# Query rotation placed a step later, key sums split by token tile, a split first output step and early first scores in a two-block transformer kernel

## The chip, the cores and the metric

The program runs on one core of a Trainium2 chip. The metric is the device time of one execution in microseconds (us); lower is better. All times below are of that core.

## What is computed

Two transformer blocks over 512 tokens of width 1024, in float32. The first has differential attention, a convolution branch and 16 experts of which each chooses its tokens. The second has an mLSTM layer, and then the layer that matters here: keys and values from a small latent vector (MLA), read by 8 heads in chunks, and a memory attention of 4 heads over 256 memory rows. The parts of the reference that the change touches:

```python
def shared_kv(x, positions, kv_norm, w_kv_a, kv_lat_norm, w_kv_b, k_gain):
    h = rmsnorm(x, kv_norm)
    c_kv, k_pe = split_cols(h @ w_kv_a, [KV_LORA, QK_ROPE])
    kv = (rmsnorm(c_kv, kv_lat_norm) @ w_kv_b).reshape(bsz, s, B_HEADS, QK_NOPE + V_HEAD)
    k_nope, v = kv[..., :QK_NOPE], kv[..., QK_NOPE:]
    k = jnp.concatenate([k_nope, jnp.broadcast_to(k_pe[:, :, None, :], ...)], axis=-1)
    k = rmsnorm(k, k_gain)
    k = jnp.concatenate([k[..., :QK_NOPE], rope(k[..., QK_NOPE:], positions)], axis=-1)
    return k, v

def mla_layer(x, positions, k_sh, v_sh, ...):
    q_lat, z, mq, mz = split_cols(h @ w_in, [Q_LORA, B_WIDTH, MEM_WIDTH, MEM_WIDTH])
    q = (rmsnorm(q_lat, q_lat_g) @ w_q_up).reshape(bsz, s, B_HEADS, QK_HEAD)
    q = rmsnorm(q, q_gain)                      # then rope on its last 64 columns
    attn = chunk_causal_attention(q, k_sh, v_sh)
    y_b = attn * jax.nn.silu(z)
    y_mem = memory_attention(mq, mz, mk, mv, mq_gain)
    return x + jnp.concatenate([y_b, y_mem], axis=-1) @ w_out
```

## The kernel before

The kernel is a sequence of stages, each a block of five instruction streams written out by hand (TensorE, VectorE, ScalarE, GpSimd, and SyncE for loads). Engines meet through semaphores inside a stage and at a barrier of all engines at its end. The last two stages matter.

**The products.** `SplitGemm` computes products in float32 quality with three faster ones: ScalarE writes the rounded operand (`highs`, L482), VectorE the rest (`lows`, L491 and L495), and TensorE multiplies high by high, high by low and low by high (`multiply`, L429). A job is one product against one block of weights; it has `k_tiles` steps of 128 rows, and units of 128 tokens or features, each with a PSUM bank. Steps of all jobs are numbered through. ScalarE and VectorE go through the same numbers (`split`), one to three steps ahead of TensorE: at each number they split the operands, then take finished units out of PSUM, then do the other work that was added for that number (`add(work, number, function)`). TensorE waits per step for the low parts (`wait_low`), and at a job's first step per unit for the bank (`wait_bank`). So the place in these lists sets the order on every engine.

**The latent stage** (`latent_stage`, barrier at L3369). Its jobs in order: the latent of keys and values (KVA, steps 0 to 7), the latent of queries (QLA, 8 to 15), four pairs of heads of keys and values (KVB + c, two steps each, 16 to 23), four pairs of heads of queries (QUP + c, three steps each, 24 to 35), the memory queries (MQ, 36 to 43), and the gates (44 to 67). Five banks, 0 to 4, go round among the units; banks 5 to 7 are for transposes. For each pair c of key heads:
- ScalarE squares the keys (L3517); VectorE sums them to 8 columns `ks[:, 0]`, 4 token tiles by 2 heads (L3675), and adds the sum of the shared rotary part `pes`, 4 columns, each for both heads (`sums_k`, L3676).
- ScalarE takes the root (L3521), VectorE inverts it (L3682, `finish_k`) and scales the rotary part (L3686); GpSimd scales the keys `kn` by it (L3747), and behind that scales up to three tiles of `xt` (L3756), the operand of the MQ job.
- TensorE transposes them (`turn_k`, L3418 and L3420) once ScalarE has taken the previous pair out (`take_k`, L3526 and L3527).

The last pair of key and value heads, KVB + 3, is taken by VectorE (L3306), with two copies per unit. For the queries, `rotate_q(c)` (four VectorE operations, L3707 to L3710) stands at the number where the job is taken, plus 1 (plus 2 for c = 0): 30, 32, 35 and 38. `sums_q(c)` (L3691) stands at plus 2, `finish_q(c)` at plus 4; TensorE turns them (`turn_q`) at plus 3.

**The attention stage** (`attention_stage`, name `ba`). It has `nu` = 48 units: 16 of memory attention, 32 of chunked attention. TensorE's loop over u issues scores of unit u (L2436), transposes of the probabilities of unit u - 4 (L2450), from u = 48 on a step of the output product, and the values product of unit u - 5 (L2460). VectorE takes the maximum (L2491), normalises (L2498) and takes the result (L2503); ScalarE does the exponential (L2550) and copies the transposed probabilities (L2535). Scores lie in banks 0, 1, 2, 7 in turn. The four first units of the output product take over these banks, so that each waits in turn for one of the last four exponentials (`bank_waits`). In the loop before:

```python
                if 4 <= u < nu + 4:
                    turn(u - 4)
                if nu <= u < nu + 4:
                    out.products(pe, start=u - nu, stop=u - nu + 1)
                if u >= 5:
                    values(u - 5)
```

Of the kernel before, what the change touches and what calls it, by code (L numbers as in the profile page):

```python
# [19 lines left out]
ALU = mybir.AluOpType  # L20
# [277 lines left out]
class SplitGemm:  # L298
# [133 lines left out]
    def products(self, pe, after=None, start=0, stop=None):  # L432

        for s in range(start, len(self.steps) if stop is None else stop):
            j, k = self.steps[s][0], self.place[s]
            job, n_units, k_tiles = self.jobs[j], self.main_units(j), self.block(j)[1]
            if k == 0 and "split_ready" in job:
                pe.wait_ge(*job["split_ready"])
            w, a = self.w_split[s % self.ns], self.split_of(s)
            self.wait_low(pe, s)  # L440
            for u in range(n_units):
                unit = self.units[self.first_unit[j] + u]
                if k == 0:
                    self.wait_bank(pe, unit)
                ins = self.multiply(pe, unit, w, a, k == 0, k == k_tiles - 1)
                if k == k_tiles - 1 and u < n_units - 1:
                    ins.then_inc(self.ready, 1)
            ins.then_inc(self.used, 1)
            for work in (after or {}).get(s, []):
                work()  # L450

    def operands(self, s):
# [1932 lines left out]


def attention_stage(m, name, units, at, st_at, y, x, out_slots, store):

# [19 lines left out]

    score_banks = (0, 1, 2, 7)
    bank_of = lambda u: score_banks[u % 4]  # L2410
# [11 lines left out]
    with nc.Block() as block:  # L2422
# [6 lines left out]
        def _(pe):  # L2429
            def scores(u):  # L2430

                if u >= 4:
                    pe.wait_ge(exped, u - 3)
                lhs, rhs = units[u]["scores"]
                alone = "turned" not in units[u]
                ins = pe.matmul(ps[:, bank_of(u), 0:units[u]["width"]], lhs, rhs, start=True, stop=alone)  # L2436
                if alone:
                    ins.then_inc(scored, 1)
# [25 lines left out]
            for u in range(nu + 5):  # L2464
# [8 lines left out]
                if 4 <= u < nu + 4:  # L2473
                    turn(u - 4)
                if nu <= u < nu + 4:
                    out.products(pe, start=u - nu, stop=u - nu + 1)
                if u >= 5:
# [4 lines left out]
        def _(dve):  # L2482
            step = m.dve_steps.on(dve)

            def head(u):
                w = units[u]["width"]
                dve.wait_ge(scored, u + 1)
                s = ps[:, bank_of(u), 0:w]
# [739 lines left out]

def latent_stage(m, x, xt, kt, kpt, qt, qpt, v, y, mqt, q_scale, slots):

# [138 lines left out]
    with nc.Block() as block:  # L3369
# [9 lines left out]
        def _(pe_):  # L3379
# [75 lines left out]
            for h in range(3):  # L3455
                add(work, taken_at(MQ) + 6, lambda h=h: turn_mq(h))
            add(work, taken_at(MQ) + 9, lambda: turn_mq(3))
            g.products(pe_, work)

# [128 lines left out]
        def _(dve):  # L3588
# [84 lines left out]
            def sums_k(c):  # L3673
                dve.wait_ge(k_squared, c + 1)
                step(nc.vector.tensor_reduce(ks[:, 0], k_junk[:], AX.X, ALU.add))  # L3675
                tt(ks[:, 0], ks[:, 0], spread(pes[:], 2), ALU.add).then_inc(k_summed, 1)  # L3676

# [54 lines left out]
            for c in range(NB):  # L3732
                add(work, taken_at(QUP + c) + (1 if c else 2), lambda c=c: rotate_q(c))
                add(work, taken_at(QUP + c) + 2, lambda c=c: sums_q(c))
# [26 lines left out]
def two_blocks(nc, dram):  # L3761
    with ExitStack() as ctx:
        ctx.enter_context(nc.allow_non_contiguous_dma("short rows of gains and gate weights"))
        m = Machine(nc, ctx, dram)
        m.gates = m.keep("gates", [CAP, NE])
        m.rows = m.keep("rows", [CAP, NE + 1], U32)
# [142 lines left out]
        q_scale = m.area("q_scale", [P, BH // 2, 4, 2], 108608)  # L3909
        latent_stage(m, x, xt, kt, kpt, qt, qpt, v, y, mqt, q_scale, m.gaps + [m.arena + 98304])  # L3910
        m.close()
# [53 lines left out]
```

## Time and profile before

| | us |
|---|---|
| median of 3 runs | 2184.02 |
| lowest and highest run | 2183.22, 2184.87 |
| the profiled execution, its own time | 2185.32 |
| its span, first to last instruction | 2183.2 |
| TensorE busy | 2157.2 |
| VectorE busy | 1653.6 |
| ScalarE busy | 1392.3 |
| GpSimd busy | 340.0 |
| TensorE clock granted (mean) | 0.999 |

PE is TensorE's multiplications, PEld its weight loads, DVE VectorE, ACT ScalarE, POOL GpSimd; a q behind a name is the engine's sequencer. L495 is line 495 of the kernel. A row of a timeline gives start, length, engine, line, operation, what it writes and reads, the shape, and how many such instructions in a row it stands for; in square brackets, where there was one, the idle time of the engine before it and who ended it. The latent stage runs from 1840 to 2033.7 in the span, the attention stage from there to the end.

### The profile page before, as it was taken

The numbers are of one execution on the slowest core, as the hardware profiler recorded it, in microseconds if no ns is written. First come the engines' busy times: TensorE is split into PE (matmuls) and PEld (weight loads), VectorE is DVE, ScalarE is ACT, GpSimd is POOL, SyncE is SP. The second block draws the span as 40 slices with busy tenths as digits, with TensorE's granted clock in tenths as the row PEclk, the third lists the DMA queues.
The fourth block names the chain that finished last, engine by engine and source line by source line (L and its number), as shares of the span: only waits on it lengthen the run. The fifth ranks groups of instructions, "written<-read, shape, count | busy, mean of one in ns | idle before, by whom it ended". The sixth has DMA issues, their size and how long they took to land. (4 is left out here: it accounts for less than half of the span.)

```text
span 2183.2 us, 31916 instructions
## 1 busy us (share of the span) xinstructions
PE 2157.2 (99%) x11509; PEld 1557.7 (71%) x11509; DVE 1653.6 (76%) x2155; ACT 1392.3 (64%) x1796; POOL 340.0 (16%) x209
## 2 busy tenths in 40 slices
PE   9999999999999999999999999999999999999999
PEld 9988765565565555655556555687897788888777
DVE  6456678998989989899898998756755556875664
ACT  5345577777777777767777777755555555676653
POOL 3032041211122111121111200330000000211000
PEclk9999999999999999999999999999999999999999
DMA  6213479999999999999999999522321131241301
GB/s 188 83 57 117 168 272 370 377 382 371 384 383 372 382 370 382 385 376 380 371 383 383 374 381 368 217 86 88 90 66 59 59 118 51 61 138 39 116 1 39
DMA packets 179672, 506.88 MB, mean 232 GB/s; under 512 B 12557, under 2 KB 57389, under 8 KB 179581
## 3 DMA queue, kind: packets, MB, share of 16 engines
q1 hardware_dynamic: 174829, 494.92, 60.8%
q0 software_dynamic: 4752, 10.75, 2.2%
q8 instruction: 57, 0.93, 0.2%
q14 instruction: 34, 0.28, 0.0%
HBM read 492.99 MB, written 10.48 MB: 231 GB/s over the span
## 5 line engine op out<-in xcount | busy, mean ns | idle before, releaser
L2252 DVE TENSOR_TENSOR pieces_low<-pieces,pieces_high 128x2048 fp32r<-128x2048 f32 x383 | 873.3, 2290 | 109.2 <-ACT pieces_high L2197 105.1
L2197 ACT ACTIVATE pieces_high<-pieces 128x2048 fp32r<-128x2048 f32 x382 | 729.1, 1917 | 237.8 <-PE ps L2121 231.2
L2121 PE MATMUL ps<-pieces_high,ex_x 128*66 128x512 f32 x2080 | 574.9, 393 | 1.1 <-PEq L1593 0.5
L2121 PEld LDWEIGHTS ps<-pieces_high,ex_x 128*66 128x66 f32 x2080 | 279.4, 136 | 195.6 <-issue 7.2
L2121 PE MATMUL ps<-pieces_low,ex_x 128*66 128x512 f32 x1040 | 323.6, 392 | 0.0
L2121 PE MATMUL ps<-pieces_high,ex_h 128*66 128x512 f32 x992 | 277.0, 393 | 0.0
L495 DVE TENSOR_TENSOR in_w<-ring,in_w 128x256 fp32r<-128x256 f32 (+2 forms) x276 | 125.1, 460 | 155.0 <-ACT in_w L482 153.1
L2593 PE MATMUL ps<-hn_split,in_w 128*128 128x512 f32 x864 | 221.3, 406 | 2.7 <-DVE in_w L495 1.6
L2121 PEld LDWEIGHTS ps<-pieces_low,ex_x 128*66 128x66 f32 x1040 | 141.6, 136 | 97.4
L482 ACT ACTIVATE in_w<-ring 128x256 fp32r<-128x256 f32 (+2 forms) x276 | 117.0, 426 | 127.2 <-PE ps L2593 57.2
L2121 PEld LDWEIGHTS ps<-pieces_high,ex_h 128*66 128x66 f32 x992 | 133.6, 136 | 90.4 <-DVE pieces_low L2252 3.2
L2593 PEld LDWEIGHTS ps<-hn_split,in_w 128*128 128x128 f32 x864 | 159.5, 188 | 44.3 <-DVE in_w L495 5.1
L429 PE MATMUL ps<-out_w,out_a 128*128 128x512 f32 x768 | 180.5, 393 | 2.2 <-DVE out_a L495 1.5
L429 PEld LDWEIGHTS ps<-out_w,out_a 128*128 128x128 f32 x768 | 142.6, 188 | 34.6 <-DVE out_a L495 3.4
L2355 POOL DMA_INDIRECT ex_rows<-xhat_scratch,ex_rows_in x15 | 110.6, 7374 | 320.3 <-DVE ex_rows_in L2258 312.8
L2361 POOL DMA_INDIRECT resid_scratch<-ex_y,ex_rows_out x15 | 73.1, 4872 | 551.3 <-DVE ex_y L2307 551.3
L2121 PE MATMUL ps<-pieces_low,ex_h 128*66 128x512 f32 x496 | 154.3, 392 | 0.0
L2121 PEld LDWEIGHTS ps<-pieces_low,ex_h 128*66 128x66 f32 x496 | 67.6, 136 | 46.8
L495 DVE TENSOR_TENSOR out_w<-ring,out_w 128x512 fp32r<-128x512 f32 x64 | 44.2, 690 | 68.9 <-ACT out_w L482 68.6
L482 ACT ACTIVATE out_w<-ring 128x512 fp32r<-128x512 f32 x64 | 40.2, 628 | 75.2 <-PE ps L429 61.3
L2601 PE MATMUL ps<-in_w,hn_split 128*128 128x256 f32 x576 | 80.4, 293 | 0.7 <-ACT mq L2665 0.7
L3747 POOL TENSOR_TENSOR kn<-kn,k_ss 128x512 f32<-128x512 f32 x8 | 11.1, 1408 | 432.2 <-DVE k_ss L3682 432.2
(510 smaller groups left out, 2777.7 us busy)
## 6 DMA issues: line engine op xcount, KB each, us to landing
pieces<-in_w_gate SPq DMA_DIRECT2D x128, 1024.0 KB, 7.3
pieces<-in_w_up SPq DMA_DIRECT2D x128, 1024.0 KB, 7.7
pieces<-in_w_down SPq DMA_DIRECT2D x128, 1024.0 KB, 8.6
ring<-in_a_w_in SPq DMA_DIRECT2D x24, 1024.0 KB, 5.2
ring<-in_b_w_in SPq DMA_DIRECT2D x4, 2048.0 KB, 7.8
ring<-in_w_in SPq DMA_DIRECT2D x7, 1024.0 KB, 4.9
ring<-in_b_w_out SPq DMA_DIRECT2D x2, 3072.0 KB, 14.3
ring<-in_w_in SPq DMA_DIRECT2D x8, 512.0 KB, 3.6
```

The lines of the kernel that those rows point to most:

```text
L429: ins = pe.matmul(self.psum(unit), lhs, rhs, start=(first and i == 0), stop=(last and i == 2))
L482: self.m.nc.scalar.activation(parts[:, 0, :], x, ACT.Copy, scale=scale).then_inc(self.high, 1)
L495: ins = self.m.nc.vector.tensor_tensor(parts[:, 1, :], x, parts[:, 0, :].bitcast(F32), ALU.subtract)
L2121: ins = pe.matmul(ps[0:CAP, banks + c, :], parts[a][:, k0 + k, :], w[b][:, k, c * 512:(c + 1) * 512], start=start and k == 0 and a == b == ...
L2197: nc.scalar.activation(m.high[:, n % NSPLIT, :], m.pieces[:, n % NPIECE, :], ACT.Copy).then_inc(high_done, 1)
L2252: nc.vector.tensor_tensor(m.low_part[:, n % NSPLIT, :], m.pieces[:, n % NPIECE, :], m.high[:, n % NSPLIT, :].bitcast(F32), ALU.subtract).t ...
L2355: nc.gpsimd.indirect_dma_start(out=xg[:], out_offset=None, in_=m.xhat[:], in_offset=bass.IndirectOffsetOnAxis(ap=rows_in[:, 0:1], axis=0)) ...
L2361: nc.gpsimd.indirect_dma_start(out=m.resid[:], out_offset=bass.IndirectOffsetOnAxis(ap=rows_out[:, 0:1], axis=0), in_=y[:], in_offset=None ...
L2593: ins = pe.matmul(psum, w[:, x, u * P:u * P + psum.shape[0]], a[:, y, :], start=(first and i == 0), stop=(last and i == 2))
L2601: ins = pe.matmul(psum[:, b, :], a[:, x, t0:t0 + P], w[:, y, 0:cols], start=(first and i == 0 and b == 0), stop=(last and i == 2 and b == ...
L3747: tt(part, part, spread(r[:, :, h], x.shape[3]), ALU.mult).then_inc(scaled, 1)
```

## The change

Four edits:
- `rotate_q(3)` stands at number 39 instead of 38, behind the splits of step 39 and ahead of `sums_q(3)`.
- `sums_k` adds the rotary sum with four tensor_scalar operations, one for each token tile, each on 2 columns with a column of `pes` as the scalar, instead of one tensor_tensor on 8 columns.
- The output product's step 0 is issued in two parts: units 0 to 2 at u = 48, unit 3 at u = 49 ahead of step 1. `products` is cut into `product(pe, s, first, stop)` for this.
- The scores of unit 0 are issued in the latent stage, behind its last product, into bank 7; the banks of the scores become 7, 0, 1, 2. A new semaphore `m.first_scored` tells VectorE of them, and `scored` counts from unit 1 on.

```diff
+    def product(self, pe, s, first=0, stop=None):
+
+        j, k = self.steps[s][0], self.place[s]
+        job, n_units, k_tiles = self.jobs[j], self.main_units(j), self.block(j)[1]
+        if k == 0 and "split_ready" in job:
+            pe.wait_ge(*job["split_ready"])
+        w, a = self.w_split[s % self.ns], self.split_of(s)
+        self.wait_low(pe, s)
+        for u in range(first, n_units if stop is None else stop):
+            unit = self.units[self.first_unit[j] + u]
+            if k == 0:
+                self.wait_bank(pe, unit)
+            ins = self.multiply(pe, unit, w, a, k == 0, k == k_tiles - 1)
+            if k == k_tiles - 1 and u < n_units - 1:
+                ins.then_inc(self.ready, 1)
+        if u == n_units - 1:
+            ins.then_inc(self.used, 1)
...
+FIRST_SCORES = 7
...
-    score_banks = (0, 1, 2, 7)
+    score_banks = (FIRST_SCORES, 0, 1, 2)
...
             def scores(u):
 
+                if u == 0:
+                    return
...
-                if nu <= u < nu + 4:
-                    out.products(pe, start=u - nu, stop=u - nu + 1)
+                if u == nu:
+                    out.product(pe, 0, stop=3)
+                elif u == nu + 1:
+                    out.product(pe, 0, first=3)
+                if nu < u < nu + 4:
+                    out.product(pe, u - nu)
...
-                dve.wait_ge(scored, u + 1)
+                dve.wait_ge(*((scored, u) if u else (m.first_scored, 1)))
...
+            def first_scores():
+                pe_.wait_ge(mq_taken, MEMH)
+                pe_.matmul(ps[:, FIRST_SCORES, 0:MEM], mqt[:, 0, 0:P], mk[:, 0, :], start=True,
+                           stop=True).then_inc(m.first_scored, 1)
+
+            add(work, len(g.steps) - 1, first_scores)
...
-                tt(ks[:, 0], ks[:, 0], spread(pes[:], 2), ALU.add).then_inc(k_summed, 1)
+                for t in range(4):
+                    ins = ts(ks[:, 0, t, :], ks[:, 0, t, :], pes[:, t:t + 1], None, ALU.add)
+                ins.then_inc(k_summed, 1)
...
-                add(work, taken_at(QUP + c) + (1 if c else 2), lambda c=c: rotate_q(c))
+                add(work, taken_at(QUP + c) + (1 if c in (1, 2) else 2), lambda c=c: rotate_q(c))
...
+        m.first_scored = m.lasting("first_scored")
```

## Rows read from the trace of the kernel before

**Rows 1.** The page's line of engines: busy us (share of the span) and number of instructions.
```profile
PE 2157.2 (99%) x11509; PEld 1557.7 (71%) x11509; DVE 1653.6 (76%) x2155; ACT 1392.3 (64%) x1796; POOL 340.0 (16%) x209
```
**Rows 2.** The timeline of TensorE in the latent stage; columns as told above.
```profile
1907.90 4.21 PE L429 MATMUL ps<-in_w,qlt 128*128 128x384 f32 x21 [0.43 <-DVE v L3306]
...
1913.93 4.47 PE L429 MATMUL ps<-in_w,qlt 128*128 128x384 f32 x24
1918.56 1.06 PE L3418 MATMUL ps<-masks,kn 128*128 128x128 f32 x8 [0.16 <-issue]
...
1940.40 5.95 PE L429 MATMUL ps<-in_w,in_a 128*128 128x512 f32 x24 [0.86 <-DVE in_a L495]
```
**Rows 3.** The timeline of all engines around the boundary of the two stages.
```profile
2030.89 2.64 ACT L3337 ACTIVATE y<-ps 128x512 f32<-128x512 f32 x4 [4.89 <-PE ps L429]
...
2033.80 1.28 ACT L2550 ACT_TABLE_LOAD   x1 [0.27 <-PEq L3369]
...
2033.83 2.58 PE L2436 MATMUL ps<-mk,mqt 128*128 128x256 f32 x10 [0.94 <-PEq L3369]
2034.54 0.86 DVE L2491 TENSOR_REDUCE ba_st<-ps 128x1 f32<-128x256 f32 x2 [7.67 <-PE ps L2436]
2035.09 0.47 ACT L2550 ACTIVATE ba_probs<-ps,ba_st 128x256 f32<-128x256 f32 x1
```
**Rows 4.** The timeline of all engines around the output product's first step.
```profile
2107.34 2.46 PE L429 MATMUL ps<-out_w,out_a 128*128 128x512 f32 x9
...
2108.68 0.48 ACT L2535 ACTIVATE ba_pt<-ps 128x384 f32<-128x384 f32 x1
...
2110.49 0.96 PE L429 MATMUL ps<-out_w,out_a 128*128 128x512 f32 x3 [0.69 <-ACT ba_probs L2550]
...
2111.29 0.60 PE L2460 MATMUL ps<-ba_pt,v 128*128 128x128 f32 x4
...
2111.97 3.02 PE L429 MATMUL ps<-out_w,out_a 128*128 128x512 f32 x12
```
**Rows 5.** VectorE at the key sums: line L3676, timeline, and one wait (total, times, longest).
```profile
L3676 DVE TENSOR_TENSOR k_ss<-k_ss,k_pe_ss x4: 169/990/1245, 1889.3 to 1913.2; 128x8 f32<-128x8 f32 x4
...
1905.72 0.99 DVE L3676 TENSOR_TENSOR k_ss<-k_ss,k_pe_ss 128x8 f32<-128x8 f32 x1
1906.64 0.55 DVE L495 TENSOR_TENSOR in_w<-ring,in_w 128x384 fp32r<-128x384 f32 x1
...
DVE k_ss L3682 <- ACT k_ss L3521: 2.5, 1, 2.5
```
**Rows 6.** The timeline of GpSimd beside the key sums of c = 2 and 3.
```profile
1905.42 1.27 POOL L3756 TENSOR_TENSOR xt<-xt,row_scales 128x512 f32<-128x512 f32 x1
1906.65 1.66 POOL L3756 TENSOR_TENSOR xt<-xt,row_scales 128x512 f32<-128x512 f32 x1
...
1914.08 1.69 POOL L3756 TENSOR_TENSOR xt<-xt,row_scales 128x512 f32<-128x512 f32 x1
```
**Rows 7.** Timelines of VectorE and GpSimd elsewhere, where both work.
```profile
1437.44 0.81 DVE L3031 TENSOR_SCALAR xl_tmp<-xl_tmp 128x16 f32<-128x16 f32 x1
...
1435.37 2.85 POOL L3221 TENSOR_SCALAR x<-fin_gained,fin_roots 128x1024 f32<-128x1024 f32 x1
...
1974.33 1.54 DVE L495 TENSOR_TENSOR in_a<-xt,in_a 128x512 fp32r<-128x512 f32 x1
1975.79 1.53 DVE L491 SCALAR_TENSOR_TENSOR in_w<-ring,cols,in_w 128x512 fp32r<-128x512 f32 x1
```
**Rows 8.** Timelines of TensorE and VectorE around the last query rotation.
```profile
1947.41 8.43 PE L429 MATMUL ps<-in_w,in_a 128*128 128x512 f32 x36
...
1948.74 0.69 DVE L495 TENSOR_TENSOR in_a<-xt,in_a 128x512 fp32r<-128x512 f32 x1
```
**Rows 9.** The timeline of ScalarE behind the key sums and copies.
```profile
1909.87 1.06 ACT L3517 ACTIVATE k_junk<-kn 128x1024 f32<-128x1024 f32 x1 [2.40 <-DVE v L3306]
...
1914.18 0.30 ACT L3521 ACTIVATE k_ss<-k_ss,eps 128x8 f32<-128x8 f32 x1 [1.19 <-DVE k_ss L3676]
```

More of the change, by code:

```diff
@@ L434, in products @@
         for s in range(start, len(self.steps) if stop is None else stop):
[L435 to L448, printed above, removed]
+            self.product(pe, s)
             for work in (after or {}).get(s, []):
                 work()
+    def product(self, pe, s, first=0, stop=None):
[14 more added lines that the diff above has]
+            ins.then_inc(self.used, 1)
     def operands(self, s):
@@ L3226, in _, with latent_stage @@
                                     ALU.mult).then_inc(s["mq_scaled"], 1)
-def latent_stage(m, x, xt, kt, kpt, qt, qpt, v, y, mqt, q_scale, slots):
+def latent_stage(m, x, xt, kt, kpt, qt, qpt, v, y, mk, mqt, q_scale, slots):
     nc, ps = m.nc, m.ps
@@ L3909, in two_blocks @@
         q_scale = m.area("q_scale", [P, BH // 2, 4, 2], 108608)
-        latent_stage(m, x, xt, kt, kpt, qt, qpt, v, y, mqt, q_scale, m.gaps + [m.arena + 98304])
+        latent_stage(m, x, xt, kt, kpt, qt, qpt, v, y, mk[1], mqt, q_scale, m.gaps + [m.arena + 98304])
         m.close()
```

## The prediction, made before the changed kernel had run

> **What bounds the kernel now.** I read the page's engine line first: TensorE is busy for 2157.2 us, so at most 26 us of this program are idle time of TensorE, and an edit can pay only where it takes a piece of these away [rows 1]. Next I read TensorE's order of time in the two stages that the diff touches, for its own waits. In the latent stage three matter: 0.43 us at 1907.90, 0.16 at 1918.56 and 0.86 at 1940.40 [rows 2]. At the boundary of the stages there is one of 0.94, and one of 0.69 in the first step of the output product [rows 3, 4]. Then I read what VectorE, GpSimd and ScalarE do ahead of each. All the rest is TensorE passing from one multiplication to the next. The profiled execution took 2185.32 us with a span of 2183.2; the median of the runs is 2184.02, 1.3 below it. The sum below is a difference within the profiled span, and I lay it on the median.
>
> **Key sums.** `sums_k(c)` ends in one addition of 8 columns. It takes 0.169 us where nothing hinders it, and 0.99 us or more in the last three of its four turns [rows 5]. The reason stands beside it: GpSimd is scaling `xt`, in instructions of 1.27 us. The addition that starts at 1905.72 ends at 1906.71, just behind GpSimd's instruction, which ends at 1905.42 + 1.27 = 1906.69 [rows 5, 6]. So the two engines share something that one of them holds for a whole instruction. The diff replaces the addition by four tensor_scalar of 2 columns each, back to back (nothing shows their spacing; at the 0.17 of the free addition, which moves as little, four take between 0.2 and 0.7, and I take 0.4).
>
> What matters is whether a tensor_scalar waits for GpSimd too. The row nearest to it says yes: 16 columns at 1437.44 take 0.81 us, where 8 columns take 0.17 when free, and end at 1438.25, where GpSimd's instruction ends at 1435.37 + 2.85 = 1438.22 [rows 7]. That row has an immediate as its scalar and another instruction on GpSimd, so it isn't proof. The Trainium skill, page Vector Engine (DVE) Microarchitecture Reference, section 5.1 Performance modes, says that a one-source operation with two fp32 elements in SBUF runs in the mode that uses both read ports, and SBUF — State Buffer, section SBUF: two separate sides, that such an operation and a GpSimd instruction lock each other out for a whole instruction. The 0.81 us agrees; no row here has 2 columns. By that rule four small instructions meet the lock four times where one addition met it once. By it the sum is the forecast's +3.1, by its opposite rival A's -0.8.
>
> How many of GpSimd's instructions do they wait for? Two rows of VectorE in a row, at 1974.33 and 1975.79, last 1.54 and 1.53 us each, where the first kind takes 0.69 when alone [rows 7, 8]: when GpSimd has its next instruction ready, it gets in between two of VectorE. Yet the L495 behind the addition starts at 1906.64, just ahead of GpSimd's next at 1906.65, and isn't held up (0.55) [rows 5, 6]. So about two short VectorE instructions pass at each change. Four tensor_scalar and the L495 behind them then pass as 2, 2, 1, over three of GpSimd's instructions instead of one.
> - c = 0: no GpSimd work runs; VectorE is 0.2 us later. TensorE has no wait nearby: nothing.
> - c = 1: the addition stands beside the second of three GpSimd instructions; one is left, 1.3 us. VectorE idles for 2.5 us before the reciprocal that follows, waiting for ScalarE [rows 5]: it covers this. Nothing.
> - c = 2: L495 starts two instructions later, 2 x 1.27 = 2.5 us. Behind it stand the eight copies that free the banks of the last key and value product. TensorE waits for them at 1907.90 already [rows 2], and ScalarE's next square has waited 2.40 us for them [rows 9]. All of the 2.5 us arrives at TensorE.
> - c = 3: two GpSimd instructions are there. The sum is ready one later, 1.27 us. ScalarE has waited 1.19 us for it at 1914.18, in front of the takes and of the turned keys for which TensorE waits at 1918.56 [rows 2, 9]. There is no slack, so 1.3 us arrive.
> Together +3.8 us.
>
> If instead the tensor_scalar doesn't wait, the gain is small: the L495 behind it has two SBUF inputs and waits for the same end, 1906.69, which is 0.05 us from where it starts now [rows 5, 6]. ScalarE gets its sum 0.6 us sooner at c = 3, but then copies four units that TensorE finishes one by one in its stretch from 1913.93, the last near 1916.2 [rows 2]. I take 0.1 us. So this edit lies between -0.1 and +3.8.
>
> **Rotation.** `rotate_q(3)` moves behind the splits of step 39. Before, these splits end at 1949.43; TensorE needs them after the first of the three steps in its 8.43 us stretch from 1947.41, at 1950.2 [rows 8]. They now end some 2 us earlier, where 0.8 of slack stood. `sums_q(3)` comes behind both, and keeps its place. The rotation ends 1.3 us later, at about 1949.4, and its reader on TensorE stands behind step 40, at 1955.7. Nothing, and the wait of 0.86 at 1940.40 belongs to `rotate_q(2)`, which isn't moved [rows 2].
>
> **First scores.** They go into the latent block. TensorE's last product there ends near 2033.83 - 0.94 = 2032.9; two short multiplications more end near 2033.4, while ScalarE's last copy ends at 2030.89 + 2.64 = 2033.53 [rows 3]. The boundary still waits for ScalarE. VectorE's first maximum can start some 0.6 us before 2034.54. But the exponential it feeds waits for the table load, 2033.80 + 1.28 = 2035.08, and starts at 2035.09 [rows 3]. VectorE's third maximum stands behind the first normalisation in the code, so nothing moves. The change of banks is a renaming. Worth 0; with bounds of -0.2 (a maximum less in the ramp) and +0.3 (TensorE late at the boundary). No DMA is moved, and the queue of the loads issues as before.
>
> **First output step in two parts.** Its fourth unit waits for the last exponential: 0.69 us idle at 2110.49; behind it come the values product of unit 43 (2111.29) and the transposes of unit 45, up to 2111.97. What they read is ready: ScalarE's copy behind the one for unit 43 already ends at 2108.68 + 0.48 = 2109.16 [rows 4]. In the change these two fill the hole. TensorE is free at 2107.34 + 2.46 = 2109.80, they take 2111.97 - 2111.29 = 0.7 us, and the fourth unit still starts at 2110.49. Step 1 starts at 2111.29 instead of 2111.97. What comes later keeps its distances and has no wait, as TensorE runs on to the end. -0.7, between 0 and -0.8.
>
> **Sum.** +3.8 + 0 + 0 - 0.7 = +3.1 us: 2184.02 + 3.1 = 2187.1.
>
> **The rivals.**
> A. The 2-column tensor_scalar doesn't wait for GpSimd. For it: it has one tensor as input, and instructions with two are what the trace mostly shows waiting. Against it: the row at 1437.44 [rows 7]. -0.1 - 0.7 = -0.8: 2183.2.
> B. They wait, but all four pass at one change. Then only L495 loses its place to one GpSimd instruction: +1.3 at c = 2, +0.2 at c = 3, -0.7: +0.8, 2184.8. For it: L495 passes right behind the addition now. Against it: the pair at 1974.33.
> C. Slower than a measurement can miss: GpSimd's instructions last 1.66 to 1.69 us, and not 1.27, wherever a VectorE instruction stands between them [rows 6]. If each change costs that, c = 2 costs 3.3 and c = 3 1.7; with 0.3 at the boundary and 0.7 back this is +4.6, 2188.6. It decides once TensorE's waits at 1907.90 and 1918.56 grow by more than 5.1 us together. Against it: the 0.4 us more are the time of the VectorE instruction itself there, and a 2-column instruction is shorter.
> D. The output step doesn't gain, as the values product waits for a VectorE row that isn't ready; +3.8, 2187.8. Speaks against it: the copy at 2108.68 ends 0.6 us before TensorE is free [rows 4].
>
> **How the numbers follow.** Forecast 0.45; A 0.27; B 0.15; C 0.07; D 0.04; 0.02 for something in the order of the program that no row shows and that gains much. The range goes from A with 0.8 us for the scatter of the runs (they span 1.65) to just short of C: 2182.4 to 2188.4. It leaves out C, the 0.02, and the tails of A and the forecast, some 0.17. 0.2% is 4.4 us, about what a measurement of this kernel can tell from no change: faster is below 2179.7, slower above 2188.4. Slower: C and a small tail of the forecast, 0.09. Faster: 0.02. Same: 0.89.
>
> **What would show each step.** Key sums: four rows in place of the addition; in the forecast the first and the third last about a microsecond each at c = 2, the L495 behind them starts near 1909.2 relative to the other rows (1906.6 in rival A), and TensorE's wait before the second unit of the first query product grows from 0.43 to about 2.9; its wait before the last turned keys grows from 0.16 to about 1.4. In rival A all four last 0.17 and the L495 takes the wait over. Output step: the 0.69 is gone and values and transposes stand between units three and four. First scores: a first maximum right behind the boundary, and an exponential that still starts with the table load's end. Rotation: no row of TensorE changes. The prediction is wrong if the sums stay short, or if TensorE's waits in the latent stage change anywhere else.

## The result, and the profile after

The changed kernel takes 2187.07 us (median of 22 runs, 2186.48 to 2189.13), the kernel before, in the same number of runs beside it, 2184.62 (2183.22 to 2186.31). The ratio is 1.0014 with an interval of 1.0008 to 1.0019: slower by 1.7 to 4.2 us, which is less than the 0.2% that the prediction took as its bound of "same". The forecast was 2187.1. Its profiled execution took 2187.21 us with a span of 2185.0; that of the kernel before took 2185.32 with 2183.2.

The page's engine line of the changed kernel stands against [rows 1]. VectorE has the twelve instructions more (2167 against 2155), and 5.2 us more of busy time, which is waiting inside the short instructions: their rows add up to 9.45 us against 3.40:

```profile
PE 2158.4 (99%) x11509; PEld 1560.2 (71%) x11509; DVE 1658.8 (76%) x2167; ACT 1393.4 (64%) x1796; POOL 338.9 (16%) x209
```

**TensorE in the latent stage** (timeline of the changed kernel), against [rows 2]:

```profile
1905.03 0.78 PE L429 MATMUL ps<-in_w,qlt 128*128 128x384 f32 x3
1908.82 6.62 PE L429 MATMUL ps<-in_w,qlt 128*128 128x384 f32 x21 [3.02 <-DVE v L3320]
1915.28 1.03 PE L3432 MATMUL ps<-masks,kn 128*128 128x128 f32 x8
...
1921.13 1.06 PE L3432 MATMUL ps<-masks,kn 128*128 128x128 f32 x8 [0.15 <-issue]
...
1942.97 5.95 PE L429 MATMUL ps<-in_w,in_a 128*128 128x512 f32 x24 [0.86 <-DVE in_a L500]
```

The wait in front of the second unit of the first query product has gone from 0.43 to 3.02 us, as forecast. But the 21 multiplications behind it now take 6.62 us where they took 4.21, and the wait before the last turned keys has not grown at all. Another wait is gone, that of 0.55 before the turned keys behind the 21 multiplications, which neither [rows 2] nor the prediction has (kernel before):

```profile
1912.67 1.06 PE L3418 MATMUL ps<-masks,kn 128*128 128x128 f32 x8 [0.55 <-issue]
```

So of the 2.41 us that the 21 multiplications lose, 1.69 reach the turned keys (distances of 6.46 and 4.77 us from the second unit). The rotation's neighbour, 0.86, is as it was.

**The key sums** on VectorE, with GpSimd and ScalarE beside them (timelines of the changed kernel), against [rows 5, 6, 9]:

```profile
1887.66 0.62 DVE L3698 TENSOR_SCALAR k_ss<-k_ss,k_pe_ss 128x2 f32<-128x2 f32 x4
...
1904.06 3.58 DVE L3698 TENSOR_SCALAR k_ss<-k_ss,k_pe_ss 128x2 f32<-128x2 f32 x4
1907.56 0.55 DVE L500 TENSOR_TENSOR in_w<-ring,in_w 128x384 fp32r<-128x384 f32 x1
1908.03 0.41 DVE L3320 COPY kn<-ps 128x256 f32<-128x256 f32 x1
...
1914.07 2.50 DVE L3698 TENSOR_SCALAR k_ss<-k_ss,k_pe_ss 128x2 f32<-128x2 f32 x4
...
1903.76 3.73 POOL L3779 TENSOR_TENSOR xt<-xt,row_scales 128x512 f32<-128x512 f32 x3
...
1913.77 2.51 POOL L3779 TENSOR_TENSOR xt<-xt,row_scales 128x512 f32<-128x512 f32 x2
...
1916.60 0.30 ACT L3542 ACTIVATE k_ss<-k_ss,eps 128x8 f32<-128x8 f32 x1 [2.70 <-DVE k_ss L3698]
```

Alone (c = 0, the first row) four additions take 0.62 us. At c = 2 they take 3.58, until GpSimd has done all of its three instructions (1903.76 + 3.73 = 1907.49), and L500 and the copies stand behind them. At c = 3 they take 2.50 us, beside two instructions of GpSimd. Taken one by one, the four of c = 2 last 0.99, 1.33, 1.31 and 0.22 us, those of c = 3 1.00, 1.32, 0.22 and 0.22: each waits for an instruction of its own as long as GpSimd has one. At c = 1, also beside GpSimd, the four take 2.75 us where the addition took 1.25; VectorE's wait for ScalarE behind them shrinks from 2.52 to 1.03 and covers that.

**The clock.** The windows of the same stretch (length, busy time of PE, PEld, DVE, ACT and POOL with counts, granted clock, share of DMA, GB/s):

```profile
1905.00:1909.00 4.00, 0.98 (x7) 0.66 (x6) 4.00 (x8) 0.71 (x2) 2.49 (x3) 0.86 0.00 0
1909.00:1914.40 5.40, 5.40 (x17) 5.40 (x18) 5.33 (x11) 3.11 (x5) 3.46 (x3) 0.50 0.10 10
1914.40:1920.00 5.60, 5.60 (x37) 5.56 (x37) 4.75 (x8) 3.31 (x8) 4.66 (x4) 0.97 0.30 99
```

In the middle window the granted clock is 0.50, the lower of the two levels (1.2 GHz in place of 2.4). The 0.86 and 0.97 beside it put the low stretch at 1907.9 to 1914.7: it began while TensorE stood in its 3.02 us wait, and lasted some 6.8 us. That is where the 21 multiplications lose their time, and no step of the prediction has it.

**The output step and the boundary** (timelines of the changed kernel), against [rows 4] and [rows 3]:

```profile
2109.95 2.45 PE L429 MATMUL ps<-out_w,out_a 128*128 128x512 f32 x9
2112.24 0.61 PE L2470 MATMUL ps<-ba_pt,v 128*128 128x128 f32 x4
2112.68 0.49 PE L2460 MATMUL ps<-masks,ba_probs 128*128 128x128 f32 x3
2113.18 3.67 PE L429 MATMUL ps<-out_w,out_a 128*128 128x512 f32 x15
2116.69 0.83 PE L2470 MATMUL ps<-ba_pt,v 128*128 128x128 f32 x6
...
2033.47 2.64 ACT L3351 ACTIVATE y<-ps 128x512 f32<-128x512 f32 x4 [4.88 <-PE ps L429]
2036.38 1.28 ACT L2564 ACT_TABLE_LOAD   x1 [0.27 <-PEq L3383]
2036.42 0.42 DVE L2505 TENSOR_REDUCE ba_st<-ps 128x1 f32<-128x256 f32 x1 [6.97 <-PEq L3383]
2037.68 0.47 ACT L2564 ACTIVATE ba_probs<-ps,ba_st 128x256 f32<-128x256 f32 x1
```

The values product and the transposes fill the hole of 0.69 us: from the first of the nine multiplications to the values product of six (2116.69 - 2109.95) it is 6.74 us. In the kernel before, the same distance is 2114.83 - 2107.34 = 7.49. At the boundary, VectorE's first maximum comes right behind the barrier, and the exponential still starts with the end of the table load, 2036.38 + 1.28.

**The sum of it.** I matched TensorE's multiplications of the two traces one by one, and read where their distance changes: +4.2 us between 1905 and 1921, -0.75 in the output step, nothing at the rotation, nothing at the boundary. That is +3.5, and yet the spans differ by 1.9. The rest, -1.7, arises about 460 us ahead of any line of the change, as the kernel before ran at half clock for a while there:

```profile
1448.00:1452.00 4.00, 4.00 (x23) 4.00 (x23) 1.11 (x6) 1.01 (x2) 0.00 (x0) 0.58 0.12 41
```

This is the kernel before; in that window the changed kernel has

```profile
1448.00:1452.00 4.00, 4.00 (x30) 3.74 (x29) 1.32 (x5) 2.29 (x5) 0.00 (x0) 1.00 0.06 21
```

The instructions are the same there, and of the thirteen kernels profiled in this study four have the lower clock in it (before, and the experiments sums_c2, sums_c3 and sums_early), nine don't, and no edit goes with it. So it differs between executions and is no part of the change, and the spans can't be compared as a whole. Below I compare stretches.

### The profile page after: what moved, and what is told of

It is laid out like the page before. It is cut to its first block and busy times, and to the rows that moved or that the text cites. A ratio compares the mean times of both kernels' runs of the same rounds, so it can differ in the third digit from the quotient of the medians.

```text
span 2185.0 us, 31930 instructions
## 1 busy us (share of the span) xinstructions
PE 2158.4 (99%) x11509; PEld 1560.2 (71%) x11509; DVE 1658.8 (76%) x2167; ACT 1393.4 (64%) x1796; POOL 338.9 (16%) x209
## 5 line engine op out<-in xcount | busy, mean ns | idle before, releaser
L500 DVE TENSOR_TENSOR in_w<-ring,in_w 128x256 fp32r<-128x256 f32 (+2 forms) x276 | 125.1, 460 | 154.2 <-ACT in_w L487 152.4
L500 DVE TENSOR_TENSOR out_w<-ring,out_w 128x512 fp32r<-128x512 f32 x64 | 44.2, 690 | 69.0 <-ACT out_w L487 68.7
```

The source lines that it names most:

```text
L500: ins = self.m.nc.vector.tensor_tensor(parts[:, 1, :], x, parts[:, 0, :].bitcast(F32), ALU.subtract)
```

## The experiments

My theory after this: (1) the key sums cost all of the loss, by the number of short instructions that meet GpSimd; (2) c = 2 costs 2.6 us through the wait, and the wait costs more through the clock; (3) the output step gives back 0.75; (4) rotation and first scores do nothing. Rivals: the sort of instruction costs, not the number; c = 3 costs as forecast and is only misplaced; the low clock is chance or comes with something other than the wait; the output step's gain needs the other edits.

The table has TensorE's time, from its timelines, between the same four points of every kernel: the start of the first unit of the first query product (1906.69 in the kernel before), its second unit (1907.90), the turned keys behind it (1912.67), and the turned keys of c = 3 (1918.56). The last columns are the medians of this kernel and of the kernel before beside it.

| kernel | to second unit | to turned keys | to those of c = 3 | sum against before | median | before |
|---|---|---|---|---|---|---|
| before | 1.21 | 4.77 | 5.89 | | | |
| after | 3.79 | 6.46 | 5.85 | +4.23 | 2187.07 | 2184.62 |
| sums_only | 3.78 | 5.62 | 6.15 | +3.68 | 2187.52 | 2184.22 |
| no_sums | 1.21 | 4.76 | 5.89 | -0.01 | 2183.52 | 2184.22 |
| sums_c2 | 3.78 | 6.47 | 5.83 | +4.21 | 2187.26 | 2184.22 |
| sums_c3 | 1.20 | 4.77 | 6.99 | +1.09 | 2185.05 | 2184.22 |
| add4 | 3.60 | 6.53 | 5.85 | +4.11 | 2187.06 | 2184.02 |
| add2 | 2.35 | 4.77 | 5.87 | +1.12 | 2185.24 | 2184.02 |
| early_scale | 1.16 | 4.77 | 5.86 | -0.08 | 2190.98 | 2184.02 |
| sums_early | 1.17 | 4.76 | 5.88 | -0.06 | 2190.18 | 2184.02 |
| fill | 3.84 | 4.77 | 7.00 | +3.74 | 2186.95 | 2184.58 |
| out_only | 1.20 | 4.77 | 5.86 | -0.04 | 2182.81 | 2184.58 |
| junk_out | 1.16 | 4.77 | 5.86 | -0.08 | 2183.45 | 2184.58 |

### The key sums alone, and all but them

sums_only is the kernel before with this edit alone:

```diff
-                tt(ks[:, 0], ks[:, 0], spread(pes[:], 2), ALU.add).then_inc(k_summed, 1)
+                for t in range(4):
+                    ins = ts(ks[:, 0, t, :], ks[:, 0, t, :], pes[:, t:t + 1], None, ALU.add)
+                ins.then_inc(k_summed, 1)
```

> The kernel before with the key sums' edit alone (four tensor_scalar). If that edit is the cause: +3.8 us by the forecast's sum (2.5 at c = 2, 1.3 at c = 3), +4.3 by the reading of the trace after (2.6 of waiting at c = 2, 1.7 because TensorE then runs at half its clock for 6.8 us, nothing more at c = 3, whose delay lies beside that). If the 2.5 us of the whole change come from another edit or from where the code lies: within 0.5 us of before.

no_sums is the changed kernel with the reverse of it, so that the three other edits stand alone.

> The changed kernel with the one addition of 8 columns put back, so with the other three edits alone. If the key sums are the whole loss: -0.7 to -0.8 us against the kernel before, all of it at the output product's first step. If the first scores or the rotation cost anything: above -0.5.

Measured: sums_only 1.0016 [1.0007, 1.0025], +3.3 us at the median; no_sums 0.9996 [0.9987, 1.0005], -0.7. In the trace of no_sums the stretch is that of the kernel before to 0.01 us, and from there to the end TensorE's distance to the kernel before changes in the output step only, by 0.73. So the sums are the whole loss, and the other three together are the output step's gain. (Further up, the low clock at 1448 that the kernel before had and no_sums had not makes 1.5 us between these two profiled executions.) sums_only shows one thing more: its low clock lasted 3.4 us and not 6.8, and began only 1.6 us behind the same wait of 3.0 (which ended at 1909.49):

```profile
1905.00:1909.00 4.00, 1.49 (x12) 1.16 (x10) 4.00 (x6) 0.65 (x2) 3.16 (x3) 1.00 0.00 0
1909.00:1914.40 5.40, 4.91 (x18) 4.53 (x19) 5.37 (x12) 3.00 (x6) 2.78 (x2) 0.69 0.01 3
```

It costs less (5.62 in the second column, not 6.46), and then 0.26 us show at c = 3 (6.15).

### One turn at a time

sums_c2 and sums_c3 put the four tensor_scalar at one turn only:

```diff
+                if c == 2:
+                    for t in range(4):
+                        ins = ts(ks[:, 0, t, :], ks[:, 0, t, :], pes[:, t:t + 1], None, ALU.add)
+                else:
+                    ins = tt(ks[:, 0], ks[:, 0], spread(pes[:], 2), ALU.add)
```

> The kernel before with four tensor_scalar for c = 2 only. By the forecast's sum +2.5 us: a wait of TensorE near 2.9 us in place of 0.43, at full clock. By the clock reading +4.3: the same wait, and then a stretch at half clock, so nearly as much as with the edit for all four c.

> The kernel before with four tensor_scalar for c = 3 only. By the forecast's sum +1.3 us, in TensorE's wait before the last turned keys (0.16 becomes 1.4), too short a wait for the clock. If the delay at c = 3 has cover, 0. By either theory the effects of c = 2 and c = 3 need not add: under the clock reading this +1.3 is real when alone, and vanishes behind c = 2.

Measured: sums_c2 1.0013 [1.0004, 1.0022], +3.0 at the median; sums_c3 1.0003 [0.9994, 1.0012], +0.8. In the traces c = 2 alone gives the whole of what the change costs, wait and low clock. c = 3 alone does cost something, and this is where (timeline of TensorE in sums_c3):

```profile
1913.51 4.76 PE L429 MATMUL ps<-in_w,qlt 128*128 128x384 f32 x24
1919.24 1.06 PE L3418 MATMUL ps<-masks,kn 128*128 128x128 f32 x8 [0.98 <-issue]
```

The wait is 0.98 where it was 0.16, and the stretch in front of it grows by 0.3; 1.09 us together. In the changed kernel this is not seen. The table tells why: at c = 2 the low clock makes TensorE 1.7 us late, while VectorE's sum at c = 3 doesn't depend on it and is only 1.1 us late. The two lie side by side and the larger counts. The sums agree: 2.6 + the larger of 1.7 and 1.1 is 4.3 (after +4.23, sums_c2 +4.21), and in sums_only, where the low clock took 0.85, 2.6 + 1.1 = 3.7 (+3.68).

### Number or sort of instruction

add4 has four tensor_tensor of 2 columns, add2 two of 4 columns, at all four turns:

```diff
-                tt(ks[:, 0], ks[:, 0], spread(pes[:], 2), ALU.add).then_inc(k_summed, 1)
+                for t in range(4):
+                    part = ks[:, 0, 1 * t:1 * (t + 1)]
+                    ins = tt(part, part, spread(pes[:, 1 * t:1 * (t + 1)], 2), ALU.add)
+                ins.then_inc(k_summed, 1)
```

> The kernel before with four tensor_tensor of 2 columns in place of the one of 8. If it is the number of instructions that counts, each losing its place to one of GpSimd's: the same as with four tensor_scalar, +3.8 to +4.3 us. If it is the kind (tensor_scalar waits longer): less than half of that.

> The kernel before with two tensor_tensor of 4 columns. If every instruction after the first waits for one more of GpSimd's (as the trace after shows: three of four waited), one more GpSimd instruction at c = 2 and c = 3 each, 1.3 us: TensorE's wait at c = 2 grows from 0.43 to 1.7. If TensorE's clock falls only behind the long wait, +2.6 at full clock at most (+1.3 at c = 2 and up to +1.3 at c = 3). If two of VectorE's pass at each change, as the forecast had it, the second one passes and only the split behind it is late.

Measured: add4 1.0014 [1.0005, 1.0024], add2 1.0007 [0.9998, 1.0016]. VectorE at c = 2 in add4:

```profile
1904.04 2.30 DVE L3678 TENSOR_TENSOR k_ss<-k_ss,k_pe_ss 128x2 f32<-128x2 f32 x4
1906.26 1.63 DVE L495 TENSOR_TENSOR in_w<-ring,in_w 128x384 fp32r<-128x384 f32 x1
```

and in add2 (two instructions):

```profile
1903.75 1.06 DVE L3678 TENSOR_TENSOR k_ss<-k_ss,k_pe_ss 128x4 f32<-128x4 f32 x2
1904.73 1.64 DVE L495 TENSOR_TENSOR in_w<-ring,in_w 128x384 fp32r<-128x384 f32 x1
```

The four tensor_tensor wait for two of GpSimd's instructions (2.30 us), the four tensor_scalar for three (3.58). The L495 that follows then waits for the third itself (1.63 instead of 0.55), so that the copies behind it start within 0.2 us of the same place in both (3.97 us behind the first addition with the tensor_scalar, 3.77 in add4). So the number counts, and the sort of instruction changes only which one does the waiting. The prediction's "two short instructions pass at each change" is what tensor_tensor does: 2, 2 and L495 in add4, 2 and L495 in add2, whose sum of c = 3 is not late at all (5.87 in the third column). tensor_scalar goes one at a time.

### Without the contention

early_scale is the kernel before with GpSimd's eight scalings of `xt` ahead of all key work. sums_early has the four tensor_scalar besides.

```diff
+            pool.wait_ge(r["spread_taken"], 1)
+            pool.wait_ge(g.low, g.low_count(2 * KD))
+            for k in range(KD):
+                tt(xt[:, k, :], xt[:, k, :], scales[:], ALU.mult).then_inc(r["scaled"], 1)
...
-                if c == 0:
-                    pool.wait_ge(r["spread_taken"], 1)
-                    pool.wait_ge(g.low, g.low_count(2 * KD))
-                for k in range(3 * c, min(3 * c + 3, KD)):
-                    tt(xt[:, k, :], xt[:, k, :], scales[:], ALU.mult).then_inc(r["scaled"], 1)
```

> The kernel before with GpSimd's eight scalings of xt moved ahead of the keys, into the time when GpSimd idles. Both theories: the addition takes 0.17 us at every c, and TensorE's wait of 0.43 us at the first query product falls away: -0.4 to -0.8 us, if VectorE's splits beside the scalings at their new place have slack; if not, up to +2 us.

> The same with four tensor_scalar in place of the addition. If their cost is the waiting for GpSimd's xt scalings, it goes with these: within 0.3 us of early_scale, and the four take some 0.6 us together at every c. If their cost is their number, or where the code lies: 2 us or more above early_scale.

Measured: 1.0029 [1.0017, 1.0041] and 1.0029 [1.0018, 1.0040], at the medians of 6 and 7 runs 7.0 and 6.2 us above the kernel before. The expectation allowed +2 at most. As a better kernel this failed; as a test of the sums it is clean. With no GpSimd work beside them the four tensor_scalar take 0.62 us at every turn, and the stretch of the table is the same with them and without (11.81 and 11.79 us). So the whole price of the sums is the contention. Why the move itself costs is to be seen further up, in VectorE and TensorE of early_scale:

```profile
1883.31 1.48 DVE L3644 TENSOR_TENSOR masks<-lat,table_cos 128x256 f32<-128x256 f32 x1
1884.71 1.38 DVE L3645 TENSOR_TENSOR k_pe_squares<-lat,masks 128x128 f32<-128x128 f32 x1
1886.02 1.37 DVE L3646 TENSOR_TENSOR k_pe_squares<-lat,masks 128x128 f32<-128x128 f32 x1
1887.42 1.37 DVE L3647 TENSOR_TENSOR masks<-masks,k_pe_squares 128x256 f32<-128x256 f32 x1
...
1890.55 4.33 PE L429 MATMUL ps<-in_w,latt 128*128 128x512 f32 x12 [3.69 <-issue]
```

The scalings now stand beside the rotation of the keys' rotary part, and four instructions of VectorE last 1.4 us each. That makes a wait of 3.69 us on TensorE, and the window 1890 to 1894 behind it has a granted clock of 0.57. It is the same pair of costs at another place: between 1885 and 1891 TensorE falls 5.3 us behind the kernel before in both traces. The rest of the 7.0 and 6.2 does not come from this stretch; early_scale has 2.4 us of it before 11 us of the span are over, where its clock was low too.

A second thing is to be read here: even without any contention TensorE waits 0.40 us for its second unit, not 0. In early_scale the copies of VectorE wait for TensorE's turned keys (L3420) at that place. So of the 0.43 of the kernel before, 0.40 was not the addition's to give.

### The wait filled with work

fill is the changed kernel, with the first unit's three multiplications issued six times:

```diff
             if k == 0:
                 self.wait_bank(pe, unit)
+            for n in range(job.get("fill", 0) if k == u == 0 else 0):
+                self.multiply(pe, unit, w, a, True, True)
             ins = self.multiply(pe, unit, w, a, k == 0, k == k_tiles - 1)
...
+    jobs[2 + NB]["fill"] = 5
```

> All of the change, and the three multiplications of the first unit of the first query product are issued six times instead of once (each time from a fresh start into the same bank, so that the result stays what it is). They stand in the hole of 3.0 us in front of the second unit: 15 multiplications at 0.18 us fill 2.7 us of it. VectorE and GpSimd do what they do in the change. Theory (the hole itself costs 2.6 us, and TensorE's standing still in it costs 1.7 us more, as the granted clock falls to half for the 6.8 us behind it): the second unit still starts some 3.4 us behind the first one's 1905.4, with a wait of about 0.4 us; the multiplications behind it start every 0.18 us again, and not every 0.32, with a granted clock near 1 between 1909 and 1914; the key sums of c = 3 then cost what they cost alone, up to 0.8 us. Against the kernel before +0.9 to +1.7 us at the median, where the change has +2.4. Rival (the clock falls for a reason that is not the idle time): half clock from 1908.8 to 1914.7 as in the change, and +2.4 at the median.

Measured: 1.0011 [1.0002, 1.0020], +2.4 us at the median. TensorE's timeline and windows:

```profile
1905.43 3.42 PE L429 MATMUL ps<-in_w,qlt 128*128 128x384 f32 x18
1909.27 4.23 PE L429 MATMUL ps<-in_w,qlt 128*128 128x384 f32 x21 [0.41 <-DVE v L3322]
...
1921.04 1.06 PE L3435 MATMUL ps<-masks,kn 128*128 128x128 f32 x8 [0.99 <-issue]
```

```profile
1905.00:1909.00 4.00, 3.85 (x25) 3.53 (x23) 4.00 (x7) 0.71 (x2) 2.93 (x3) 1.00 0.02 4
1909.00:1914.40 5.40, 4.60 (x25) 3.94 (x26) 5.37 (x11) 3.11 (x5) 3.01 (x3) 1.00 0.00 0
```

The second unit starts as late as in the change (3.84 us behind the first), and the low clock is gone: 4.23 us for the 21 multiplications and a granted clock of 1.00, against 6.62 and 0.50. In this execution the low clock is gone with the idle time, and the idle time is all that was taken away. And at once the cost of c = 3 comes out, with a wait of 0.99. What I had expected for the total was wrong: I took 1.7 us off for the clock and put 0.8 on for c = 3, counted from the median. In the trace it is -1.7 and +1.15, so the low clock costs the change only 0.5 us net (4.23 against 3.74), and a median doesn't tell 0.5 us.

One profiled execution of each kernel doesn't show that the wait always brings the low clock. But every run of these kernels has its mean granted clock on record. A low stretch of 3.4 us makes it 0.999 (the kernel before, profiled) and one of 6.8 us 0.998 (the changed kernel, profiled); a mean that rounds to 1.0 leaves room for 2.2 us at half clock, so for neither. The record doesn't say where in a run the stretch lay. The numbers of runs:

| kernels | 1.0 | 0.999 | 0.998 or less |
|---|---|---|---|
| before, in the experiments' three series | 45 | 38 | 1 |
| no_sums, sums_c3, add2, out_only, junk_out | 35 | 18 | 2 |
| fill | 7 | 4 | 0 |
| after | 7 | 10 | 5 |
| sums_only, sums_c2, add4 | 6 | 14 | 13 |
| early_scale, sums_early | 0 | 3 | 10 |

Where TensorE has the wait of about 3 us (after, sums_only, sums_c2, add4), 42 of 55 runs show a low stretch somewhere, and 18 show 0.998 or less; where it has none, fill among them, 63 of 150 and 3. So the wait makes the low clock more frequent, but it isn't certain; fill, with 4 of 11, stands with the kernels that have no such wait, as it should if the idle time is the cause (11 runs alone would be few to tell by). Of the changed kernel, 7 of 22 runs had no low stretch. Of the two kernels with a wait of 3.7 us all 13 runs had one.

### The output step alone, and sums with no addition

out_only is the kernel before with `product(s, first, stop)` and the first output step in two parts, and nothing else.

> The kernel before with the first output step in two parts, and nothing else of the change. Theory (this edit brings all that the change gives back, the rotation and the first scores bring nothing): -0.7 us, the 0.69 us wait in front of the fourth unit is gone, values and transposes between units three and four. The kernel with the three other edits and the old key sums measured -0.7. Rival (rotation or first scores bring or cost something): this one stands apart from that -0.7 by 0.3 us or more in the shift of TensorE's rows.

Measured: 0.9991 [0.9982, 1.0000], -1.8 us at the median. In the trace, values and transposes stand between units three and four, and the distance from the nine multiplications to the product of six is 2111.93 - 2105.17 = 6.76 us against 7.49: -0.73, as in the changed kernel and in no_sums. So the gain is this edit's own, and since no_sums with all three edits gives the same, nothing is left for rotation and first scores. The median's -1.8 is more than the trace accounts for; its interval reaches from 0 to -3.9 and holds the 0.7, and among the runs with a mean clock of 1.0 alone it is -1.2 (2182.46 against 2183.61).

junk_out has this output step too, and key sums that need no addition: the array of the squares gets a 129th column per head which holds the rotary part's sum.

```diff
-                nc.scalar.activation(k_junk[:], kn[c % 2][:], ACT.Square, scale=QKH ** -0.5).then_inc(k_squared, 1)
+                nc.scalar.activation(k_junk[:, :, :, 0:NOPE], kn[c % 2][:], ACT.Square, scale=QKH ** -0.5).then_inc(k_squared, 1)
...
-                step(ts(pes[:], pes[:], 1.0 / QKH, None, ALU.mult))
+                ts(k_junk[:, :, :, NOPE], spread(pes[:], 2), 1.0 / QKH, None, ALU.mult)
...
-                step(nc.vector.tensor_reduce(ks[:, 0], k_junk[:], AX.X, ALU.add))
-                tt(ks[:, 0], ks[:, 0], spread(pes[:], 2), ALU.add).then_inc(k_summed, 1)
+                nc.vector.tensor_reduce(ks[:, 0], k_junk[:], AX.X, ALU.add).then_inc(k_summed, 1)
```

> The kernel before with the first output step in two parts, and with key sums that need no addition at all: the squares' array gets a 129th column per head that holds the position part's sum, divided already, and the reduction runs over 129 columns. VectorE has one short instruction less between the reduction and the L495 behind it. Theory (L495 and the rotation behind it have two inputs in SBUF and wait for the same GpSimd instruction that the addition waits for): the wait at 1907.90 stays within 0.2 us of its 0.43, ScalarE has its sum of c = 3 about 0.8 us sooner and waits that much less, TensorE's 0.16 at 1918.56 shrinks by 0.15 at most; -0.7 to -0.9 us together. Rival (the addition's wait was what TensorE waited for): 0.3 at 1907.90 is gained besides, -1.0 to -1.3.

Measured: 0.9996 [0.9987, 1.0005], -1.1 us. The L500 behind the reduction takes over the wait, whole:

```profile
1903.44 1.21 DVE L3684 TENSOR_REDUCE k_ss<-k_junk 128x8 f32<-128x1032 f32 x1
1904.68 1.39 DVE L500 TENSOR_TENSOR in_w<-ring,in_w 128x384 fp32r<-128x384 f32 x1
```

TensorE's wait goes from 0.43 to 0.38, the 0.16 of c = 3 stays. So taking the addition away altogether is worth 0.08 us here: at this place there was nothing to win, and 4 us to lose.

Of the two kernels, and of all that ran, out_only has the lowest median, 2182.81 us; the intervals of no_sums and junk_out, which have the same output step, overlap with its own.

## Why the prediction was right or wrong

**Key sums at c = 2**: forecast 2.5 us, measured 2.58. The mechanism is the one named, and that the small tensor_scalar waits for GpSimd (against rival A) is shown by the rows of 3.58 and 2.50 us. Rival B (all four pass at one change) falls with the same rows. Rival C wanted each of GpSimd's instructions to grow to 1.66 us; its three take 3.73 us together, 1.26 to 1.28 each. The inner count was wrong: tensor_scalar passes one at a time, not 2, 2, 1. The end comes out the same only because GpSimd had three instructions there. With the right count but more GpSimd work the sum would have been too small.

**Key sums at c = 3**: forecast 1.3, measured 1.1 where it stands alone (sums_c3, fill). In the profiled execution of the change it is 0 (the wait that was forecast at 1.4 is 0.15), because TensorE is late by then anyway. The two turns were simply added, and that holds only while nothing between them makes TensorE late by itself.

**c = 0 and c = 1**: nothing, as forecast. The four take 0.62 us when free, in the forecast's bounds of 0.2 and 0.7 though not its 0.4, and at c = 1 they are 1.5 us late (forecast 1.3), covered by the wait that the prediction named.

**The clock**: the missed term. The forecast has a 2.9 us wait on TensorE and says nothing on what a wait of that length does. Where it is low for 6.8 us it takes 1.7 us, of which 0.5 is left beside c = 3; in 7 of the 22 runs it wasn't low for so long anywhere. Forecast for both sums +3.8, measured +4.2 with the low clock, +3.7 without it (fill). The sum also passes over the wait of 0.55 at 1912.67: it is gone in the change (in fill it is back, with 0.53), and by the prediction's own last sign a wait of TensorE that changes elsewhere in the latent stage speaks against it.

**Rotation**: nothing, as forecast. The splits of step 39 end at 1950.01, 0.58 us later by the span and 2.0 us earlier by TensorE, which is 2.57 us later there (1942.97 against 1940.40).

**First scores**: 0, as forecast. The first maximum stands 0.7 us earlier against the boundary (forecast 0.6), and the exponential waits for the table load as before.

**Output step**: forecast -0.7, measured -0.75. Rival D falls with it.

**The total**: +3.1 forecast, +3.5 by the stretches of the profiled executions, +2.45 at the median with 1.7 to 4.2 as its interval. The record of the clocks explains most of this. The runs of the changed kernel without a low stretch have a median of 2186.71 us (7 runs); those of the kernel before in the experiments' three series have 2183.59 (45 runs; 2183.57, 2183.61 and 2183.61 in the single series). That is +3.1, what the forecast adds up to without any clock, and the stretches without it give 2.58 + 1.1 - 0.75 = +2.9. The low stretch elsewhere, as at 1448, lifts the kernel before by 1.4 us in the runs that have it (2184.99, 38 of 84), so that its median of 2184.62 stands 1.0 above its level without one, and that of the changed kernel only 0.4. (The clocks of the 22 runs of the kernel before beside the changed one aren't on record, so that this share is taken from the other series.) sums_c2 agrees, with +2.3 at full clock (3 runs) where its wait is +2.6, and sums_c3 with +1.4 (9 runs) where it has +1.1.

So the forecast's terms are those of an execution without the low clock. The clock is the term it lacks, and where it comes, the delay of c = 3 is covered beside it. That the forecast time stands within 0.1 us of the median is luck in part: it was laid on a median of three runs that is itself 0.4 above the level at full clock, and the low clock, which the forecast doesn't have, lifts the changed kernel's median by as much.

## What to carry to other kernels

Where VectorE and GpSimd work beside each other, the number of VectorE's instructions is the price and not their size (shown here for 2 to 8 columns): a rewrite that cuts one short instruction into four pays up to four of GpSimd's instructions, and all that is queued behind them on VectorE comes later too. When a sum of costs makes TensorE wait for about 3 us, add the low clock that may follow, and when two delays reach TensorE one behind the other, ask whether the first already covers the second. Before a wait is taken away, look which row would take it over: here the next instruction of the same queue did, whole.

## What the runs showed of the hardware

**Order between the two engines.** A tensor_scalar of 2 columns (0.22 us free, and started every 0.13 us when nothing hinders) waits for one whole GpSimd instruction each, 1.3 us, as long as GpSimd has the next one ready. Of tensor_tensor of 2 or 4 columns, two go at each change of GpSimd's. I don't know why they differ; no experiment here tells. The Trainium skill, page SBUF — State Buffer, section SBUF: two separate sides, says of a GpSimd operation and a VectorE operation that uses both ports, or that has two inputs in SBUF, that whichever starts first holds the shared ports for its whole instruction and the other is blocked in full. The 3.58 and 2.50 us rows agree with that. Two others, by this profile, do not: while GpSimd has its one instruction of 2.85 us from 1435.37 [rows 7], two tensor_tensor of 256 columns on VectorE (L495, at 1436.43 and 1437.10) take 0.41 and 0.42 us, as when nothing hinders them. So the rule held for GpSimd's tensor_tensor here, and not for every operation of GpSimd's.

**The clock after a wait.** A wait of 2.85 to 3.7 us of TensorE was followed by a granted clock of 0.50 for 3.4 or 6.8 us (which cost 0.85 or 1.7 us at the stretch of the table) in the profiled executions of all six kernels that had one (after, sums_only, sums_c2, add4, early_scale, sums_early), but by the runs' mean clocks not in every execution. After 1.57 us (add2), after 1.85 (out_only, at 1390) and after 0.41 (fill) it stayed at 1.00. The Trainium skill, page TensorE: Matmul & The Clock Gate, section What's actually happening, says that the clock is gated to 1.2 GHz when the engine was idle and opened again by activity, and that the gate's own rhythm is independent of the kernel. The two lengths after the same 3.0 us wait agree with this, and so do the 7 of 22 runs of one kernel without a low stretch of such a length. The lower clock at 1448, in four profiles of thirteen, comes without a wait; ahead of it TensorE works on multiplications of 4 columns, 20 of them in 2.29 us at 1445.63 in the kernel before. Whether these are the reason no run here tells. early_scale has one more, at 9.27 for 3.4 us, when TensorE had been waiting for loads (1.36 us, then 0.35).
